# A two-block transformer kernel: queries' and values' weight units change places, and the first decay of a gated scan is worked out between them

## The reference

```python
lb_all = jnp.cumsum(jax.nn.softmax(hg_lb_logits, axis=0), axis=0)[:N_EVEN]      # the decay's lower bounds
fg = lbd + (1.0 - lbd) * jax.nn.sigmoid(f_pre)      # per head and direction; k = 1 - fg, log f = log(fg)
def step(state, inp):                               # a chunk of 32 tokens
    qc, kc, vc, gc = inp
    bcum = jnp.cumsum(gc, axis=2)
    btot = bcum[:, :, -1:]
    qe, ke = qc * jnp.exp(bcum), kc * jnp.exp(-bcum)
    att = jnp.where(causal_in_chunk, jnp.einsum('bhtk,bhsk->bhts', qe, ke), 0.0)
    o = jnp.einsum('bhtk,bhkv->bhtv', qe, state) + jnp.einsum('bhts,bhsv->bhtv', att, vc)
    kd = kc * jnp.exp(btot - bcum)
    return jnp.exp(btot)[:, :, 0, :, None] * state + jnp.einsum('bhsk,bhsv->bhkv', kd, vc), o
```

## Time and profile before

| what | value |
|---|---|
| median of 3 runs | 1751.65 us (1751.22 to 1752.39) |
| the profiled execution: its own time | 1753.42 us |
| its span in the trace | 1751.6 us |
| PE busy | 1604.5 us, 92% of the span |
| PE weight loads | 1471.6 us, 84% |
| VectorE busy | 1003.1 us, 57% |
| ScalarE busy | 691.8 us, 39% |
| mean granted PE clock | 0.946 |

### The profile page before, as it was taken

How to read it: one execution, slowest core, us unless ns; L and a number is a source line. 1 busy time by engine, 2 the same in 40 slices (tenths; PEclk the granted TensorE clock), 3 DMA queues, 4 the chain that set the end, 5 groups by cost and what they waited for, 6 DMA issues and landing times. The chain is left out here.

```text
span 1751.6 us, 29166 instructions
## 1 busy us (share of the span) xinstructions
PE 1604.5 (92%) x12106; PEld 1471.6 (84%) x12106; DVE 1003.1 (57%) x1404; ACT 691.8 (39%) x820; POOL 18.3 (1%) x40
## 2 busy tenths in 40 slices
PE   6979889999799889999679989899999989889997
PEld 6876689999777689999467766867999989889997
DVE  5574656666643366666644554444766666666665
ACT  5343433434343444344433542233443443343432
POOL 0000000000200000000000000000000000000000
PEclk9997999999899999999789987899999999999999
DMA  5331635445534735545114454502344534435451
GB/s 223 127 120 72 235 126 193 176 184 192 127 145 183 274 122 192 190 178 206 42 54 164 193 192 163 190 21 97 145 177 182 190 130 162 158 119 204 171 188 49
DMA packets 39490, 273.90 MB, mean 156 GB/s; under 512 B 4784, under 2 KB 5936, under 8 KB 6768
## 3 DMA queue, kind: packets, MB, share of 16 engines
q1 hardware_dynamic: 37296, 264.26, 40.7%
q0 software_dynamic: 1392, 5.77, 1.4%
q10 hardware_dynamic: 720, 2.68, 0.4%
HBM read 271.64 MB, written 1.05 MB: 156 GB/s over the span
## 5 line engine op out<-in xcount | busy, mean ns | idle before, releaser
L1417 PE MATMUL L<-h_hi,whi 128*128 128x256 f32 (+1 forms) x2096 | 623.7, 298 | 55.2 <-DVE h_lo L849 17.8
L1417 PE MATMUL L<-h_lo,whi 128*128 128x256 f32 (+1 forms) x2096 | 617.4, 295 | 0.0
L1417 PE MATMUL L<-h_hi,wlo 128*128 128x256 f32 (+1 forms) x2096 | 617.1, 294 | 0.0
L1417 PEld LDWEIGHTS L<-h_hi,whi 128*128 128x128 f32 x2096 | 416.8, 199 | 72.6 <-issue 66.6
L1417 PEld LDWEIGHTS L<-h_lo,whi 128*128 128x128 f32 x2096 | 416.9, 199 | 3.8
L1417 PEld LDWEIGHTS L<-h_hi,wlo 128*128 128x128 f32 x2096 | 415.8, 198 | 4.2
L800 DVE TENSOR_TENSOR wlo<-raw,whi 128x2048 fp32r<-128x2048 f32 x107 | 244.9, 2290 | 138.3 <-ACT whi L445 138.1
L919 DVE TENSOR_TENSOR wlo<-raw,whi 128x2048 fp32r<-128x2048 f32 x96 | 219.8, 2290 | 115.3 <-ACT whi L545 115.3
L445 ACT ACTIVATE whi<-raw 128x2048 fp32r<-128x2048 f32 x107 | 202.5, 1902 | 62.3 <-PE L L1417 34.4
L1417 PE MATMUL D<-hd_hi,whi 128*128 128x256 f32 x704 | 199.7, 284 | 6.4 <-DVE hd_lo L940 6.4
L1417 PE MATMUL D<-hd_hi,wlo 128*128 128x256 f32 x704 | 199.4, 283 | 0.0
(11 more groups left out here) (253 smaller groups left out, 1959.6 us busy)
## 6 DMA issues: line engine op xcount, KB each, us to landing
raw<-in_units SPq DMA_DIRECT2D x251, 1024.0 KB, 4.8
arena<-in_relx POOLq DMA_DIRECT2D x12, 128.0 KB, 4.0
arena<-in_nax POOLq DMA_DIRECT2D x1, 1536.0 KB, 6.7
t<-in_mem ACTq DMA_DIRECT2D x1, 1024.0 KB, 7.8
x<-in_x ACTq DMA_DIRECT2D x1, 1024.0 KB, 12.3
arena<-in_ctx POOLq DMA_DIRECT2D x1, 1024.0 KB, 5.0
out<-t SPq DMA_DIRECT2D x8, 128.0 KB, 2.0
arena<-in_relx POOLq DMA_DIRECT2D x12, 64.0 KB, 4.1
```

The source lines that it names most:

```text
L1417: ins = mm(dst, w[a], h[b], start=start and n == 0, stop=stop and n == 2, skip_group_check=True)
```

## The change

Units `e_hi0` (values) and `e_hq0` (queries) change places in the stream and on TensorE. On VectorE `forget(0)` and `decays(0)` come before the copies of `e_hi0`, `decayed(0)` between its two halves, and `values(0)` after them; the loop of passes starts at 1. TensorE waits for the copy of `e_hi0` no longer ahead of the scan, but in pass 0 ahead of the state products. The bounds `lb` are made in layer 1: three operations of VectorE and the exponential ahead of the attention, four more operations after `ffn1`. The two clearings of the masks stay where they were in VectorE's list, now right behind the queries' copy.

```diff
--- before.py
+++ after.py
@@ -60,7 +60,7 @@
     ("ada_a", 8, "ada", None), ("mk1", 1, "fm", "ctx"), ("mv1", 1, "tm", "ctx"), ("a_out", 4, "fm", "mix"), ("ffn0", 3 * NI, "ffn", "lat"),
     ("kv_k0", 1, "fm", "lat"), ("b_qm", 1, "fm", "lat2"), *beside(B_BESIDE, "ada_b"),
     ("b_out", 4, "fm", "mix"), ("ffn1", 3 * NI, "ffn", "lat"),
-    ("e_ff0", 1, "fm2", "both"), ("e_fb0", 1, "fm2", "both"), ("e_hi0", 1, "tm2", "both"), ("e_hq0", 1, "fm", "lat"),
+    ("e_ff0", 1, "fm2", "both"), ("e_fb0", 1, "fm2", "both"), ("e_hq0", 1, "fm", "lat"), ("e_hi0", 1, "tm2", "both"),
     ("e_ff1", 1, "fm2", "both"), ("ada_h0", 3, "ada", None),
     ("e_hg0", 1, "fm", "lat"), ("e_hq1", 1, "fm", "lat"), ("ada_h1", 3, "ada", None),
     ("e_fb1", 1, "fm2", "both"), ("ada_h2", 3, "ada", None),
@@ -668,6 +668,8 @@
             apply(col=T)
             jobs("kv_k0")
             jobs("b_qm")
+            act.wait_ge(R["lb_in"], 1)
+            A.activation(lb[:, 0:2], lb[:, 0:2], ACT.Exp).then_inc(R["lb_exp"], 1)
             attention(T_B, len(T_A), 2, NARROW, BESIDE_B)
             upto(JOBS["b_out"][0].unit + 1)
             jobs("b_out", lambda n, j: square(x, n))
@@ -695,10 +697,7 @@
 
             jobs("e_ff0", lambda n, j: f_sig(0, n if j.half == 0 else 1))
             jobs("e_fb0", lambda n, j: f_sig(1, n if j.half == 0 else 1))
-            jobs("e_hi0")
             jobs("e_hq0", lambda n, j: silu(hq[:, 0:2, :]))
-            act.wait_ge(R["lb_in"], 1)
-            A.activation(lb[:, 0:2], lb[:, 0:2], ACT.Exp).then_inc(R["lb_exp"], 1)
             for e in range(2 * HGH + 2):
                 s = e % 2
                 if e < 2 * HGH:
@@ -1176,12 +1175,25 @@
                     stores[JOBS[f"kv_k{n}"][0]] = store_k(n)
                 stores[JOBS[f"kv_v{n}"][0]] = store_v(n)
                 stores[JOBS[f"b_q{n}"][0]] = store_q(n)
+            lg = vc("hg_lb", 0, 16).rearrange("p (l d h) -> p l d h", l=2, d=2)
+            step(V.tensor_tensor(lb[:, 2], lg[:, 0], lg[:, 1], ALU.max))
+            sync()
+            step(V.tensor_tensor(lb[:, 0], lg[:, 0], lb[:, 2], ALU.subtract))
+            V.tensor_tensor(lb[:, 1], lg[:, 1], lb[:, 2], ALU.subtract).then_inc(R["lb_in"], 1)
             attention(T_B, len(T_A), 2, MIX["ml"], NARROW, BESIDE_B, stores, {5: mask_band})
             upto(JOBS["b_out"][0].unit + 1)
             residual("b_out")
             stat()
             apply(lambda k: vc("ffn_g", KB + k))
             ffn("ffn1", 1, CAUSAL3)
+            dve.wait_ge(R["lb_exp"], 1)
+            step(V.tensor_tensor(lb[:, 3], lb[:, 0], lb[:, 1], ALU.add))
+            sync()
+            step(V.reciprocal(lb[:, 3], lb[:, 3]))
+            sync()
+            step(V.tensor_tensor(lb[:, 2], lb[:, 0], lb[:, 3], ALU.mult))
+            sync()
+            step(V.tensor_scalar(lb[:, 3], lb[:, 2], -1.0, 1.0, ALU.mult, ALU.add))
 
 
             def modulation(layer, gains):
@@ -1208,22 +1220,7 @@
             apply(lambda k: gain[:, 1, k:k + 1], shift=lambda k: mod[:, 0, k, 0:1])
             for d, name in ((0, "e_ff0"), (1, "e_fb0")):
                 jobs(name, lambda n, j, b, d=d: V.tensor_copy(hf[d][:, n, :], b[:]))
-            jobs("e_hi0", lambda n, j, b: V.tensor_copy(hv[:, 2 * n:2 * n + 2, 0:256], pair(b[:])))
             jobs("e_hq0", lambda n, j, b: V.tensor_copy(hq[:, 0:2, :], pair(b[:])))
-
-            lg = vc("hg_lb", 0, 16).rearrange("p (l d h) -> p l d h", l=2, d=2)
-            step(V.tensor_tensor(lb[:, 2], lg[:, 0], lg[:, 1], ALU.max))
-            sync()
-            step(V.tensor_tensor(lb[:, 0], lg[:, 0], lb[:, 2], ALU.subtract))
-            V.tensor_tensor(lb[:, 1], lg[:, 1], lb[:, 2], ALU.subtract).then_inc(R["lb_in"], 1)
-            dve.wait_ge(R["lb_exp"], 1)
-            step(V.tensor_tensor(lb[:, 3], lb[:, 0], lb[:, 1], ALU.add))
-            sync()
-            step(V.reciprocal(lb[:, 3], lb[:, 3]))
-            sync()
-            step(V.tensor_tensor(lb[:, 2], lb[:, 0], lb[:, 3], ALU.mult))
-            sync()
-            step(V.tensor_scalar(lb[:, 3], lb[:, 2], -1.0, 1.0, ALU.mult, ALU.add))
             step(V.memset(s_am[0], 0.0))
             step(V.memset(s_am[1], 0.0))
             sync()
@@ -1315,9 +1312,14 @@
                 b = bank(j)[:]
                 V.tensor_copy(homes[j], b if j.kind == "fm2" else pair(b)).then_inc(job_evac, 1)
 
+            forget(0)
+            decays(0)
+            jobs("e_hi0", lambda n, j, b: V.tensor_copy(hv[:, 2 * n:2 * n + 2, 0:256], pair(b[:])), {0: lambda: decayed(0)})
+            upto(H_BESIDE[0][-1].unit)
+            dve.wait_ge(job_evac, stored("e_hi0"))
             values(0)
             passes = 2 * HGH
-            for i in range(passes + 3):
+            for i in range(1, passes + 3):
                 if i < passes:
                     forget(i)
                 if i >= 4 and i % 2 == 0:
@@ -1354,7 +1356,7 @@
                     upto(H_BESIDE[i][-1].unit)
                 if i == passes:
                     upto(JOBS["e_nq"][1].unit)
-                if i and i % 2 == 0 and i < passes:
+                if i % 2 == 0 and i < passes:
                     values(i // 2)
             upto(JOBS["e_nq"][0].unit + 1)
             modulation(1, [(3, 8, 0, "mix_w2", KB), (4, 32, 0, "ffn_w2", KB)])
@@ -1726,9 +1728,8 @@
             pe.wait_ge(R["mod_ready"], 1)
             jobs("e_ff0", fresh=True)
             jobs("e_fb0")
+            jobs("e_hq0")
             jobs("e_hi0")
-            jobs("e_hq0")
-            pe.wait_ge(job_evac, stored("e_hi0"))
 
             def head_sums(h):
                 pe.wait_ge(R["hg_sq"], 2 * h + 2)
@@ -1750,8 +1751,8 @@
                 pe.wait_ge(R["hg_kdt"], e + 1)
                 if d == 0:
                     pe.wait_ge(R["hg_vb"], 8 * h + 8)
-                if e == 4:
-                    pe.wait_ge(job_evac, stored("e_hi1"))
+                if e % 4 == 0:
+                    pe.wait_ge(job_evac, stored("e_hi0" if e == 0 else "e_hi1"))
 
                 for tb in range(2):
                     mm(Dn[1][:, 0:P], s_kt[:, 2 + tb, :], hv[:, 2 + tb, h * P:h * P + P], start=tb == 0,
@@ -1842,7 +1843,7 @@
         ffn_units(up[0][:, FF:], up[0][:, :FF], a["ffn_w_down"][0]),
         np.stack([kv[0], bw[3]] + [by_name[n] for n in dict.fromkeys(side)]), units(a["b_w_out"][0]),
         ffn_units(up[1][:, FF:], up[1][:, :FF], a["ffn_w_down"][1]),
-        ev[4][:1], ev[5][:1], ev[6][:1], ev[3][:1], ev[4][1:], ada[1][:3], ev[7][:1], ev[3][1:], ada[1][3:6],
+        ev[4][:1], ev[5][:1], ev[3][:1], ev[6][:1], ev[4][1:], ada[1][:3], ev[7][:1], ev[3][1:], ada[1][3:6],
         ev[5][1:], ada[1][6:9], ev[6][1:], ada[1][9:12], ev[7][1:], ev[1][:1], ada[1][12:18], ev[1][1:], ada[1][18:],
         ev[0], ev[2], units(a["ev_w_out_2"][0]),
         ffn_units(up2[0][:, :FF], up2[0][:, FF:], a["ffn_w_down_2"][0]),
```

## The result

| | us |
|---|---|
| before, median of 4 runs | 1751.43 (1750.88 to 1752.39) |
| changed, median of 4 runs | 1734.71 (1733.85 to 1739.13) |
| ratio | 0.9909, 95% interval 0.9892 to 0.9926 |
| changed, six more runs | 1733.98 (1728.21 to 1738.75) |

Faster by 16.7 us. Forecast were 14.2, that is 1737.4 us, with a range of 1734.5 to 1740.5. The profiled execution of the changed kernel took 1734.97 us, its span 1733.1. With the runs beside the experiments the kernel before has 66 runs, median 1751.5, between 1743.7 and 1756.7: its spread is wider than the three runs that the prediction had. Ten of the 66 took 1743.7 to 1746.5, with a mean granted clock of 0.950 to 0.953; those above 1750 that ran beside the experiments had 0.944 to 0.949.

A forecast was written before the change was run, and what follows sets the result against it. TensorE, busy 92%, was taken as the bound, with an 11.6 us wait before the scan and a lowered clock after it. Gap 11.7 plus clock 2.5 gave 14.2: 1751.65 to 1737.4 us, range 1734.5 to 1740.5.

The forecast's parts named there:

- the gap: TensorE's idle stretch ahead of the scan: the two starts, 11.90 us apart, come to 0.2, gain 11.7.
- one of its own signs of being wrong: End of the eighth pass: prediction wrong if the shift of 14 us isn't found unchanged there.
- The bound and the chain: Ahead of the scan: TensorE's 11.6 us wait on a VectorE-ScalarE chain gets hidden behind `e_hi0`, 3.6 us to spare.
- What is late next: Pass 0: transposed keys and `values(0)` ready about 905.9, TensorE needs them at 909.4, spare 3.5 us.
- The clock in pass 0: First product to state products: 10.20 us comes to 7.7 at full clock, gain 2.5.
- The bounds in layer 1 cost nothing: Layer 1 attention and after `ffn1`: added operations lie in idle time; with no cover they cost 1.6 us.
- The later passes are shifted as a whole: Passes after pass 0: loads follow TensorE, so everything moves earlier, waits included, with no further gain counted.
- one stretch fewer at the lower clock: Scan passes: one slow stretch fewer than now, 2.5 us each, time 1734.9; chance 0.07.
- The chain was not late: Rival, ahead of the scan: chain grows by over 3.6 us; if by 8, time 1741.8 to 1744.3; chance 0.05.
- The gain was not given back: Rival, later passes: loads that don't follow TensorE bind one, the shift ends, time 1751.6; chance 0.02.
- the unbroken start did not bring the lower clock to later passes: Rival, following passes: each loses 2.5 us at the lower clock, seven cost 17.5, time 1755.0; chance 0.02.
- the clock gives another sum: Rival, scan passes: one slow stretch more gives 1739.9, chance 0.11; one fewer 1734.9, chance 0.07.

The follow-up runs named there:

- experiment 3: Changed kernel with first gate, sum and products put behind both copies of `e_hi0`, units still swapped and bounds moved: 1748.86 us, ratio 0.9991.
- experiment 4: Changed kernel with units in their old order, values then queries, and only SiLU and the last products behind the queries' copy: 1741.92 us, ratio 0.9951.
- experiment 6: Changed kernel with ten idle VectorE memsets between the first gate and the first sum: 1734.11 us, ratio 0.9918.
- experiment 7: Changed kernel with 23 idle VectorE memsets between the first gate and the first sum: 1740.62 us, ratio 0.9954.
- experiment 5: Kernel before with 44 idle matmuls of 512 columns in TensorE's wait ahead of the scan: 1746.98 us, ratio 0.9984.
- experiment 1: Changed kernel with the bounds put back between the queries' copy and the first gate: 1734.56 us, ratio 0.9912.
- experiment 2: Kernel before with the bounds made in layer 1 and no other change: 1748.01 us, ratio 0.9982.
- experiment 8: Changed kernel run once more, unedited, for the spread and a second profile: 1733.98 us, ratio 0.9910.
- experiment 12: Changed kernel with 7 idle matmuls of 512 columns on TensorE right ahead of the scan: 1732.76 us, ratio 0.9902.
- experiment 9: Changed kernel with 13 idle matmuls in TensorE's load wait in pass 1 and 10 in its ScalarE wait in pass 4: 1725.26 us, ratio 0.9853.
- experiment 10: Changed kernel with the first job of passes 1 and 4 ahead of the ada unit instead of behind it: 1725.08 us, ratio 0.9853.
- experiment 11: Changed kernel with the first job of passes 1 to 7 ahead of the ada unit instead of behind it: 1719.96 us, ratio 0.9826.

## Why the prediction was right, point by point

**How far right.** The time of 1734.71 lies in the range, but only 0.2 above its lower end, and over ten runs 1734.4 is 0.1 below that end: that the range held is in part luck. What the prediction worked out, the gap and pass 0, came to 11.77 + 2.63 = 14.4 where 14.2 were forecast. But one of its own signs of being wrong came: the shift of 14 us was not unchanged at the end of the eighth pass. The outputs of pass 7 start at 1074.62 instead of 1093.04, 18.42 earlier, or 17.0 without the 1.41 from ahead of the scan. The 2.6 us between are the term that it had wrong, below.

**The bound and the chain.** Right: the 11.6 us wait went, and 11.77 were gained where 11.7 was forecast. The copies' spacing of 5.76, the products' end 3.6 us ahead of TensorE, and the copy of the values' first half in between all stand in the new trace. Experiments 3, 4, 6 and 7 show the three parts it needs: gate, sum and exponentials early, the queries' unit early, and a room of 3.6 (3.55 in experiment 7).

**What is late next.** Right: the keys' copy at 903.87 + 0.58 = 904.45 was 3.4 ahead of 907.83 (forecast 3.5).

**The clock in pass 0.** Right: 2.63 for 2.5, and experiment 5 gives 2.56 without touching the gap.

**The bounds in layer 1 cost nothing.** Right by the two rows above, and they bring nothing in this order either (experiment 1), which the prediction's chain implied but did not say: of its 3.6 us to spare, 2.2 come from moving the bounds.

**The later passes are shifted as a whole.** This is the term that was mis-sized: put at nothing, it measured 2.6. So much of the 18.5 us between the spans lies in passes 1 to 5, and over ten runs the median is 3.0 under the forecast, near the value of the rival "one stretch fewer at the lower clock", 1734.9, to which I had given 0.07. What differs is the clock, not the waits: in pass 4 TensorE waits 2.31 and 0.95 in the kernel before, 2.47 and 0.87 in the changed one. Stretches in pass 4 (first product to state products) and from pass 5's outputs to pass 6, first of the kernel before, then of the changed one, then of the one with only the bounds moved (experiment 2), and last pass 4 of experiment 5:

```profile
1007.05:1021.99 14.94, 11.67 (x83) 9.88 (x79) 5.64 (x16) 6.83 (x14) 0.00 (x0) 0.77 0.73 282
...
1048.27:1054.84 6.57, 6.57 (x41) 5.14 (x41) 5.35 (x13) 4.88 (x7) 0.00 (x0) 0.54 0.37 151
```

```profile
991.48:1005.18 13.70, 10.36 (x82) 8.56 (x79) 5.79 (x16) 6.97 (x14) 0.00 (x0) 0.88 0.79 307
1031.46:1036.45 4.99, 4.99 (x41) 3.56 (x41) 4.99 (x13) 4.26 (x6) 0.00 (x0) 0.72 0.49 200
```

```profile
999.87:1013.55 13.68, 10.41 (x82) 8.62 (x79) 4.95 (x14) 6.13 (x12) 0.00 (x0) 0.88 0.80 308
1039.83:1044.75 4.92, 4.92 (x41) 3.49 (x41) 4.92 (x13) 4.26 (x6) 0.00 (x0) 0.73 0.44 181
```

```profile
1002.74:1017.65 14.91, 11.62 (x82) 9.83 (x79) 5.10 (x15) 6.29 (x13) 0.00 (x0) 0.77 0.71 282
```

The number of matmuls is the same (one record is missing), the granted clock is 0.77 and 0.54 against 0.88 and 0.72. The third kernel has the old order and yet the short stretches, if in the fastest of its twelve runs, so they are no property of the new order alone. All five profiles with the new order, no wait ahead of the scan and no edit in the later passes have them (the changed kernel's own and those of experiments 1, 6, 8 and 12). The long pass 4 (14.6 to 15.1) stands in the profiles of before and of experiments 3, 4, 5 and 7. In experiment 5 pass 0 took 7.64, so a long pass 4 doesn't need a low clock in pass 0. Why the clock is down for less of the later passes stays open: experiment 12 shows only that a shift of 1.6 us doesn't undo it. That the clock falls in passes 1 and 4 at all is due to TensorE's waits for the load and for ScalarE there: filled (experiment 9, but for 1.3 us in pass 4) or taken away (experiment 10), they leave it at 1.00.

**The rivals.** The chain was not late; the price of 1.38 us for a drain at a table switch (the Trainium skill, "ScalarE: Activation LUTs", What ACT_TABLE_LOAD costs) doesn't show in the changed kernel either: the logarithm stands at 891.61, 1.3 behind SiLU's end (889.66 + 0.63), with one load in between. The gain was not given back, and the unbroken start did not bring the lower clock to later passes. The reason given against "the clock gives another sum", that three runs lie within 1.2 us, did not hold: the 66 runs of the same kernel lie within 13, and they differ in the granted clock.

## What to carry to other kernels

A chain over two side engines that TensorE waits for cost twice here: the gap, 11.8 us, and part of the pass behind it at the lower clock, 2.6. It was hidden by letting jobs whose result is needed later run between its start and its end, and by asking which single input stands last in the chain; work out the room to spare from the copies' spacing, because that tells which further savings (here the bounds) are worth nothing. Look next at the waits of 2 to 3 us that remain inside dense work: here they cost more than their length, and moving a job ahead of the unit that waits for a load brought another 14 us. And take more than three runs before you call the spread small.

## What was not expected of the hardware

- Idle matmuls made the kernel faster: 23 of them in two waits took it from 1734.4 to 1725.3, and 7 of them on the path, 1.6 us, cost nothing that the runs show (1732.8).
- A wait of 2.8 us (experiment 4) let the clock fall and stretched pass 0 from 7.57 to 9.24; in pass 1 waits of 0.3 and 3.1 us and the lower clock behind them made 14.4 us of the 8.1 that the same matmuls take in experiment 10, without a wait and at a clock of 1.00.
- Where the clock falls takes few values. Pass 4 took 13.7 to 13.9 us or 14.6 to 15.1 in the eleven profiles that leave it unedited. The last feed-forward part, hundreds of us behind the scan, took 202.7 us in twelve of the profiles and 201.25 in two (experiments 9 and 11), though nothing was edited in it.
